# A two-block transformer kernel on one core: where each attention's value products stand on TensorE

## The chip, the cores and the metric

The kernel is one program on one core of a Trainium2 chip. The metric is the device time of one execution in microseconds, as the median of several runs. The program is written engine by engine: TensorE, ScalarE (ACT), VectorE (DVE), GpSimd and the DMA queue of SyncE each have a fixed list of instructions, and they meet only at counting semaphores.

## The reference

Two transformer blocks run one after the other on 512 tokens of width 1024 (the first block adds 16 meta tokens, so it has 528). Everything is float32. The three attentions, which the change touches, are:

```python
# block 1, forgetting attention, 8 heads of 64, causal ("fox")
s = q @ k.T * scale + c[t] - c[s];  p = softmax(s);  o = p @ v
# block 1, stick-breaking attention, 8 heads of 64, causal ("sb")
z = q @ k.T * scale
a = exp(log_sigmoid(z) + later_sum_of(log_sigmoid(-z)));  o = a @ v
# block 2, grouped-query attention, 8 heads on 2 key/value heads, not causal ("gqa")
s = rope(norm(q)) @ rope(norm(k)).T * scale;  p = softmax(s);  o = p @ v
```

Around them stand the input projections, gates, output projections, the two feed-forward nets and, in block 2, a bidirectional mLSTM with a convolution.

## The kernel before, in words

Large products are made in three passes of rounded high and low parts (`three`, L585 to L588). ACT rounds a weight chunk to its high part (`split`, L1578), DVE makes the low part (`split`, L2303), and TensorE waits for the low part.

Each attention is cut into units. A unit is 128 queries of a pair of heads; in fox and sb, which are causal, it has 1 to 4 blocks of 128 keys, and units 0 and 1 are small ones for the last 16 tokens. There are 18 units in fox, 18 in sb and 16 in gqa. One unit goes through these steps:

- scores (S): TensorE, two products of 64 rows each (L768, L888, L1200), in fox and sb followed by 128-row products that add a bias or mask (L771, L773, L891);
- the weights: in fox DVE's least value (L2424), ACT's exponentials (L1721), reciprocal and scaling (L2431, L2433, L1734); in gqa L2788, L1974, L2804, L2806, L1985; in sb sigmoids on ACT and scans on DVE (L1781, L2495, L2499);
- turns T0 and T1 (L790, L909, L1215): transposes of the first and the second head's weights, both into PSUM bank 6, so T1 waits for ACT's copy of T0 (L1729, L1788, L1981), and the next unit's T0 waits for DVE's copy of T1 (L2444, L2508, L2800);
- values (V): TensorE, products into 64 columns each (L824, L928, L1231), summed over the key blocks into bank 7. In fox's and sb's units 0 and 1 they are products of 32 columns (L801). After four units, a pair of heads is complete and ACT and DVE copy it out of bank 7 (in gqa L2087 and L2859).

The loops interleave the steps of neighbouring units with pieces of a large product, the "fill", so that TensorE has work while ACT and DVE make the weights. The order on TensorE in iteration n, with the number of the unit in brackets:

- fox: S(n), T0(n-1), fill, V(n-2), T1(n-1). The fill has 48 products up to n = 8 and 24 for most of the later ones (n = 13 has 64 small ones, L719).
- sb: fill, V(n-2), T0(n-1), S(n+1), T1(n-1).
- gqa: S(u+1), first half of the fill, T0(u), V(u-1), second half, T1(u). After T1(8) come 16 small transposes (L1281); the next fill half waits for ACT's copy of them (L2091).

In gqa, ACT's order in an iteration is: evacuate the last fill, exp(u+1), in some iterations a weight split, copy of T0(u), scale the next weights. DVE's is: greatest of the scores u+1, in some iterations a low-part split, gate or convolution work, reciprocal and scaling of u+1, copy of T1(u). So the copy of T0(u) stands behind the exponentials of the scores that TensorE made at the head of the same iteration.

Of the kernel before, what the change touches and what calls it, by code (L numbers as in the profile page):

```python
# [6 lines left out]
F = mybir.dt.float32  # L7
R = mybir.dt.float32r
ALU = mybir.AluOpType
ACT = mybir.ActivationFunctionType  # L10
# [6 lines left out]
T2 = 512  # L17
# [244 lines left out]
def build(nc, W, XT, VECS, CONS, ROPE, OUT):  # L262
    with ExitStack() as ctx:
# [172 lines left out]
        def bank(b, n, rows=slice(0, P), off=0):  # L436
            return psf[rows, 512 * b + off:512 * b + off + n]
# [7 lines left out]
        def gq_split(u):  # L445

            return AT["o2", 0] + (0 if u == 0 else (u + 1) // 2) if u == 0 or (u % 2 == 1 and u <= 13) else None
# [129 lines left out]
        def _(pe):  # L577
# [199 lines left out]
            def fox_turn(n, x):  # L777

                if x == 0:
                    pe.wait_ge(S["fx_na"], n + 1)  # L780
                    pe.wait_ge(S["fx_pd"], n)
                else:
                    pe.wait_ge(S["fx_nb"], n + 1)
                    pe.wait_ge(S["fx_pa"], n + 1)
                b = fxb[n % 2]
                if n < 2 and x == 1:
                    ins = pe.transpose(bank(6, P, slice(0, 16)), b[:, 1, 0:16], C("id"))
                else:
                    for j in range(4 if n < 2 else (n - 2) % 4 + 1):
                        ins = pe.transpose(bank(6, P, off=128 * j), b[:, x, 128 * j:128 * j + 128], C("id"))  # L790
                ins.then_inc(S["fx_tr"], 1)
# [55 lines left out]
            for n in range(20):  # L847
                if n < 18:
                    fox_scores(n)
                if 1 <= n <= 18:  # L850
                    fox_turn(n - 1, 0)
                if n < 18:
                    fill_a(n)
                if n >= 2:
                    fox_values(n - 2)
                if 1 <= n <= 18:
                    fox_turn(n - 1, 1)


            HQ = (TQ // 2, TQ // 2)  # L860
# [117 lines left out]
            for n in range(20):  # L978
                if n in (2, 3):
                    fill_b(n, (0,))  # L980
                    sb_values(n - 2, range(2))
                    fill_b(n, (1,))
                    sb_values(n - 2, range(2, 4))
                elif n < 19:
                    fill_b(n)
                else:
                    fill_b(n, (0,))
                if n >= 4:
                    sb_values(n - 2)
                if n == 19:  # L990
                    fill_b(n, (1,))
                if 1 <= n <= 18:
                    sb_turn(n - 1, 0)
                if n + 1 < 18:
                    sb_scores(n + 1)
                if 1 <= n <= 18:
                    sb_turn(n - 1, 1)
# [338 lines left out]
            rope_turn(4)  # L1336
            v5_first(1, (2, 3))
            for u in range(17):
                if u < 15:
                    gqa_scores(u + 1)  # L1340
                beside_attention(u, 0)
                if u < 16:
                    gqa_turn(u, 0)
                if u >= 1:
                    gqa_values(u - 1)
                beside_attention(u, 1)
                if u < 16:
                    gqa_turn(u, 1)
                if u == 8:
                    gate_columns()  # L1350
                if u == 15:
                    prep(0, 0)
                    prep(0, 1)
                if u == 16:
                    for piece in (4, 2, 3, 5):
                        prep(0, piece)
# [211 lines left out]
        def _(ac):  # L1568
# [390 lines left out]
            def evac_v5(c, t):  # L1959
                if t % 2:  # L1960
                    ac.wait_ge(S["mm_v5"], 5 + t if c == 0 else 10 + 2 * t)
                    ac.activation(v2[:, t, 322 * c:322 * c + 322], bank(t if c == 0 else (13 + t) % 2, 322), ACT.Copy
                                  ).then_inc(S["ev_v5_a"], 1)
# [96 lines left out]
            rope_eps(4)  # L2060
            gqa_normalise(0)
            evac_v5(0, 3)
            for u in range(17):
                if u >= 1:
                    beside_attention(u - 1)
                if u == 13:
                    split(gq_split(u))
                if u < 15:
                    gqa_exp(u + 1)
                if gq_split(u) is not None and u != 13:  # L2070
                    split(gq_split(u))
                if u == 2:
                    for d in range(2):
                        ac.activation(mrow[d][:, :], con[:, 0:T2], ACT.Copy, scale=0.0).then_inc(S["mr_hi"], 1)
                if u == 6:
                    for d in range(2):
                        ac.wait_ge(S["row_t"], 4 * d + 3)
                        ac.wait_ge(S["mr_hi"], 2)
                        ac.activation(mrow[d][0:4, :], rowt[3 * d + 1][:, :], ACT.Copy).then_inc(S["mr_hi"], 1)
                if u < 16:  # L2080
                    gqa_turned(u)
                if u < 15:
                    gqa_normalise(u + 1)
                if u >= 4 and u % 4 == 0:
                    p = u // 4 - 1
                    ac.wait_ge(S["gq_pv"], 4 * p + 4)
                    ac.activation(yah[:, p, :], bank(7, T2), ACT.Copy).then_inc(S["o_hi"], 1)  # L2087
                if u == 8:
                    ac.wait_ge(S["gt_d"], 6)
                    ac.wait_ge(S["mr_lo"], 2)  # L2090
                    ac.activation(ncol[:, :].rearrange("p (d h i) -> p d i h", d=2, h=4),  # L2091
                                  bank(1, 32, off=32).rearrange("p (d i h) -> p d i h", d=2, h=4), ACT.Exp, scale=-1.0
                                  ).then_inc(S["gt_a"], 5)
                if u == 14:
                    conv_silu((0, 4, 1, 5))
                if u == 15:
                    conv_silu((2, 6, 3, 7))
                    for k in range(4):
                        ac.wait_ge(S["ev_o2"], k + 1)
                        ac.activation(sig[:, k, :], sig[:, k, :], ACT.Tanh, scale=0.5).then_inc(S["o2_s"], 1)  # L2100
                    ac.preload_act_table_set(EXPLN)
                    prep(0, 0)
                    prep(0, 1)
                    split(AT["wo2a", 0])
                if u == 16:
                    beside_attention(16)
# [188 lines left out]
        def _(dv):  # L2295
# [530 lines left out]
            rope_tile(4)  # L2826
            gqa_normalise(0)
            evac_v5(0, 2)
            for u in range(17):
                if u < 15:  # L2830
                    gqa_most(u + 1)
                if gq_split(u) is not None:
                    split(gq_split(u))
                if 1 <= u <= 5:
                    gate_rows(u - 1)
                if u == 5:
                    dv.wait_ge(S["r_y"], 15)
                    for i in range(2):
                        dv.memset(cv[i], 0.0).then_inc(S["cv_z"], 1)
                if 6 <= u <= 13:  # L2840
                    evac_conv(u - 6)
                if 14 <= u:
                    evac_v5(1, u - 14)
                if u < 15:
                    gqa_normalise(u + 1)
                if u < 16:
                    gqa_turned(u)
                if u == 8:
                    dv.wait_ge(S["mm_gt"], 2)
                    dv.tensor_copy(gcol[:, :], bank(1, 32)).then_inc(S["gt_d"], 6)  # L2850
                if u == 16:
                    dv.wait_ge(S["o2_s"], 4)
                    for k in range(4):
                        dv.tensor_scalar(sig[:, k, :], sig[:, k, :], 0.5, 0.5, ALU.mult, ALU.add).then_inc(S["o2_s"], 1)
                    split(AT["wo2a", 0])
                if u >= 4 and u % 4 == 0:
                    p = u // 4 - 1
                    dv.wait_ge(S["o_hi"], 7 + p)
                    dv.tensor_tensor(yal[:, p, :], bank(7, T2), yah[:, p, :].bitcast(F), ALU.subtract  # L2859
                                     ).then_inc(S["o_lo"], 1)  # L2860
                if u == 7:
                    for d in range(2):
                        dv.wait_ge(S["mr_hi"], 3 + d)
                        dv.tensor_tensor(mrow[d][32:36, :], rowt[3 * d + 1][:, :], mrow[d][0:4, :].bitcast(F), ALU.subtract
                                         ).then_inc(S["mr_lo"], 1)
# [455 lines left out]
```

## Time and profile before

| what | value |
|---|---|
| time, median of 3 runs | 1535.72 us (1535.66 to 1537.25) |
| span of the profiled execution | 1536.3 us |
| TensorE matmul busy | 1483.9 us, 97% |
| VectorE busy | 1025.0 us, 67% |
| ScalarE busy | 655.3 us, 43% |
| mean granted TensorE clock | 0.995 |

The profile gives no separate time for the profiled execution; its span from first to last instruction, 1536.3 us, lies between the shown runs. A row of the timeline gives start, length, engine, source line, what is written and read, and a count; several like instructions in a row are merged. Matmul ends are modelled and overlap the next start, so what a piece of work costs TensorE is read from start to start, not from its length. Float32 products with 64 rows or columns appear as two or more matmul records each.

### The profile page before, as it was taken

To read this page: it belongs to the slowest core of one execution; us is meant where nothing else is said; L and a number is where in the kernel's file an instruction comes from. 1 tells how busy PE (TensorE), PEld (TensorE's weight loads), DVE (VectorE), ACT (ScalarE), POOL (GpSimd) and SP (SyncE) were. 2 spreads that over 40 slices of the span, in tenths; PEclk is the share of its full clock that TensorE was granted. 3 is DMA by queue.
4 is the path that set the end of the run, shared out by engine and by line. 5 is a ranking of instruction groups with operands and counts; after the bars stand their busy time and mean duration, and the time that the engine had idled before them with its cause. 6 is when DMAs were issued, how large, how long until landed. Compare 5 with 4: busy or idle time off the path is not lost.

```text
span 1536.3 us, 27973 instructions
## 1 busy us (share of the span) xinstructions
PE 1483.9 (97%) x11804; PEld 1312.1 (85%) x11804; DVE 1025.0 (67%) x1446; ACT 655.3 (43%) x1052; POOL 23.3 (2%) x20
## 2 busy tenths in 40 slices
PE   7999999999998999999999899999989999999998
PEld 7998878889997999999778667768667999998876
DVE  5543447875536977777665776676778888885454
ACT  4433443342334212212343555546646555554343
POOL 0000000000000000000000020000000000000000
PEclk9999999999999999999999999999999999999999
DMA  5131024443232233232344212110112233322222
GB/s 182 57 111 56 15 70 159 149 141 117 97 110 77 103 110 131 103 107 100 131 165 154 73 54 106 55 36 28 42 42 111 83 110 110 111 94 79 91 95 83
DMA packets 37708, 147.76 MB, mean 96 GB/s; under 512 B 4304, under 2 KB 4432, under 8 KB 27856
## 3 DMA queue, kind: packets, MB, share of 16 engines
q1 hardware_dynamic: 36288, 142.76, 26.9%
q8 instruction: 94, 1.54, 0.4%
q10 hardware_dynamic: 1152, 2.16, 0.4%
q0 software_dynamic: 144, 1.05, 0.2%
q14 instruction: 30, 0.25, 0.0%
HBM read 143.86 MB, written 2.10 MB: 95 GB/s over the span
## 4 chain that ended last, share of the span: by engine, by line
PE 82%; DVE 9%; ACT 5%; issue 2%; DMA 1%; POOL 0%; ACTq 0%; DVEq 0%; SPq 0%
PE ps L586 19%; PE ps L588 18%; PE ps L587 18%; PE ps L1527 4%; PE ps L1525 4%; PE ps L1526 4%; ACT t L1578 2%; DVE t L2303 2%; PE ps L622 1%; PE ps L623 1%; PE ps L624 1%; PE ps L1231 1%; DMA t<-in_XT 1%; PE ps L1200 1%; PE ps L790 1%
## 5 line engine op out<-in xcount | busy, mean ns | idle before, releaser
L586 PE MATMUL ps<-t 128*128 128x258 f32 (+4 forms) x2160 | 688.5, 319 | 23.9 <-DVE t L2351 9.1
L588 PE MATMUL ps<-t 128*128 128x258 f32 (+4 forms) x2160 | 677.0, 313 | 0.0
L587 PE MATMUL ps<-t 128*128 128x258 f32 (+4 forms) x2160 | 675.4, 313 | 0.0
L586 PEld LDWEIGHTS ps<-t 128*128 128x128 f32 (+1 forms) x2160 | 406.8, 188 | 68.5 <-issue 16.7
L588 PEld LDWEIGHTS ps<-t 128*128 128x128 f32 (+1 forms) x2160 | 406.6, 188 | 26.9
L587 PEld LDWEIGHTS ps<-t 128*128 128x128 f32 (+1 forms) x2160 | 407.5, 189 | 24.1
L2303 DVE TENSOR_TENSOR t<-t 128x1024 fp32r<-128x1024 f32 (+2 forms) x121 | 205.6, 1699 | 211.5 <-ACT t L1578 211.5
L1578 ACT ACTIVATE t<-t 128x1024 fp32r<-128x1024 f32 (+2 forms) x121 | 174.0, 1438 | 196.2 <-PE ps L588 173.2
L1527 PE MATMUL ps<-t 128*128 128x256 f32 x504 | 142.6, 283 | 0.0
L1525 PE MATMUL ps<-t 128*128 128x256 f32 x504 | 142.5, 283 | 0.1
L1526 PE MATMUL ps<-t 128*128 128x256 f32 x504 | 141.3, 280 | 0.0
L1526 PEld LDWEIGHTS ps<-t 128*128 128x128 f32 x504 | 95.9, 190 | 0.0
L1525 PEld LDWEIGHTS ps<-t 128*128 128x128 f32 x504 | 94.6, 188 | 0.3 <-issue 0.3
L1527 PEld LDWEIGHTS ps<-t 128*128 128x128 f32 x504 | 94.2, 187 | 0.0
L3078 DVE TENSOR_TENSOR t<-t 128x1024 fp32r<-128x1024 f32 (+1 forms) x78 | 78.6, 1014 | 21.2 <-ACT t L2222 21.1
L1894 ACT ACTIVATE t<-t 128x512 f32<-128x512 f32 x22 | 13.9, 632 | 153.0 <-DVE t L2651 153.0
L2222 ACT ACTIVATE t<-t 128x1024 fp32r<-128x1024 f32 (+1 forms) x78 | 68.7, 889 | 7.1 <-PE ps L588 4.2
L2526 DVE SCALAR_TENSOR_TENSOR t<-t 128x512 f32<-128x512 f32 x84 | 62.8, 747 | 4.8 <-DMA t<-in_W 2.0
L2640 DVE TENSOR_TENSOR t<-ps,t 128x516 f32<-128x516 f32 x44 | 30.4, 691 | 43.8 <-PE ps L588 40.6
L2621 DVE TENSOR_TENSOR t<-t 128x512 fp32r<-128x512 f32 x88 | 56.6, 684 | 1.2 <-ACT t L1883 1.2
L1883 ACT ACTIVATE t<-t 128x512 fp32r<-128x512 f32 x88 | 50.0, 617 | 3.2 <-DVE t L2658 3.2
L3066 DVE TENSOR_TENSOR t<-t 128x512 f32<-128x512 f32 x72 | 49.5, 688 | 1.3
(326 smaller groups left out, 1740.8 us busy)
## 6 DMA issues: line engine op xcount, KB each, us to landing
t<-in_W SPq DMA_DIRECT2D x75, 1024.0 KB, 4.8
t<-in_W SPq DMA_DIRECT2D x62, 512.0 KB, 3.3
t<-in_W SPq DMA_DIRECT2D x100, 256.0 KB, 3.7
t<-in_W SPq DMA_DIRECT2D x4, 644.0 KB, 3.8
t<-in_XT ACTq DMA_DIRECT2D x8, 264.0 KB, 8.9
out<-t SPq DMA_DIRECT2D x8, 256.0 KB, 2.7
t<-in_ROPE POOLq DMA_DIRECT2D x1, 1024.0 KB, 5.3
t<-in_CONS SPq DMA_DIRECT2D x1, 423.0 KB, 12.2
```

Source lines behind the costliest of these rows:

```text
L586: pe.matmul(out, wh, xh, start=first, stop=False)
L587: pe.matmul(out, wh, xl, start=False, stop=False)
L588: return pe.matmul(out, wl, xh, start=False, stop=last)
L1525: pe.matmul(out, wh, xh[:, k, :], start=(k == 0 and b in (0, 1)), stop=False, skip_group_check=True)
L1526: pe.matmul(out, wh, xl[:, k, :], start=False, stop=False, skip_group_check=True)
L1527: ins = pe.matmul(out, wl, xh[:, k, :], start=False, stop=(k == 3), skip_group_check=True)
L1578: ac.activation(whi[:, n % 2, o:o + width], wraw[:, n % 2, 0:width], ACT.Copy).then_inc(S["w_hi"], 1)
L2222: ins = ac.activation(wfh[:, at:at + 512 * len(r)], src[:, a:a + 512 * len(r)], ACT.Copy)
L2303: dv.tensor_tensor(wlo[:, n % 2, o:o + width], wraw[:, n % 2, 0:width], whi[:, n % 2, o:o + width].bitcast(F), ALU.subtract).then_inc(S["w ...
L2526: dv.scalar_tensor_tensor(out=x, in0=raw(n)[:, :], scalar=condc[:, k:k + 1], in1=x, op0=ALU.mult, op1=ALU.add).then_inc(S["a_acc"], 1)
L2621: dv.tensor_tensor(al[v % 4][:, :], src[:, v % 22, :], ah[v % 4][:, :].bitcast(F), ALU.subtract).then_inc(S["an_lo"], 1)
L3078: ins = dv.tensor_tensor(wfl[:, at:at + w_], src[:, a:a + w_], wfh[:, at:at + w_].bitcast(F), ALU.subtract)
```

## The change

In fox, the values move from behind the fill to behind T1, so that they stand ahead of the next scores. In sb, they move from ahead of T0 to behind it, ahead of the scores. In gqa, they move from behind T0 to the head of the next iteration, ahead of the scores. The last iterations of each loop keep the old order. In gqa, the values of unit u - 2 now come at the head of iteration u, and ACT's and DVE's copies of a complete pair of heads move from the end of iteration 4p + 4 to iteration 4p + 5: ACT's ahead of the exponentials, DVE's behind the greatest-value reduction and ahead of the split. No instruction is added or removed.

```diff
@@ TensorE, fox
-                if n >= 2:
+                if n == 19:
                     fox_values(n - 2)
                 if 1 <= n <= 18:
                     fox_turn(n - 1, 1)
+                if 2 <= n <= 18:
+                    fox_values(n - 2)
@@ TensorE, sb
-                if n >= 4:
+                if n == 19:
                     sb_values(n - 2)
-                if n == 19:
                     fill_b(n, (1,))
                 if 1 <= n <= 18:
                     sb_turn(n - 1, 0)
+                if 4 <= n <= 18:
+                    sb_values(n - 2)
                 if n + 1 < 18:
                     sb_scores(n + 1)
@@ TensorE, gqa
             for u in range(17):
+                if u >= 2:
+                    gqa_values(u - 2)
                 if u < 15:
                     gqa_scores(u + 1)
                 beside_attention(u, 0)
                 if u < 16:
                     gqa_turn(u, 0)
-                if u >= 1:
+                if u == 16:
                     gqa_values(u - 1)
@@ ScalarE, gqa
+            def gqa_out(p):
+                ac.wait_ge(S["gq_pv"], 4 * p + 4)
+                ac.activation(yah[:, p, :], bank(7, T2), ACT.Copy).then_inc(S["o_hi"], 1)
+
             for u in range(17):
                 if u >= 1:
                     beside_attention(u - 1)
                 if u == 13:
                     split(gq_split(u))
+                if u >= 5 and u % 4 == 1:
+                    gqa_out(u // 4 - 1)
                 if u < 15:
                     gqa_exp(u + 1)
...
-                if u >= 4 and u % 4 == 0:
-                    p = u // 4 - 1
-                    ac.wait_ge(S["gq_pv"], 4 * p + 4)
-                    ac.activation(yah[:, p, :], bank(7, T2), ACT.Copy).then_inc(S["o_hi"], 1)
+                if u == 16:
+                    gqa_out(3)
@@ VectorE, gqa
+            def gqa_low(p):
+                dv.wait_ge(S["o_hi"], 7 + p)
+                dv.tensor_tensor(yal[:, p, :], bank(7, T2), yah[:, p, :].bitcast(F), ALU.subtract
+                                 ).then_inc(S["o_lo"], 1)
+
             for u in range(17):
                 if u < 15:
                     gqa_most(u + 1)
+                if u >= 5 and u % 4 == 1:
+                    gqa_low(u // 4 - 1)
                 if gq_split(u) is not None:
                     split(gq_split(u))
...
+                if u == 16:
+                    gqa_low(3)
```

## Rows read from the trace of the kernel before

**Rows 1.** The page's chain that ended last, shares by engine.
```profile
PE 82%; DVE 9%; ACT 5%; issue 2%; DMA 1%; POOL 0%; ACTq 0%; DVEq 0%; SPq 0%
```

**Rows 2.** Windows over fox, sb and gqa: us, busy of each engine, clock, DMA.
```profile
94.00:220.00 126.00, 122.17 (x1197) 104.95 (x1195) 52.37 (x95) 50.62 (x122) 0.00 (x0) 1.00 0.11 39
220.00:366.00 146.00, 143.10 (x1495) 123.42 (x1492) 104.87 (x140) 57.14 (x87) 0.00 (x0) 1.00 0.46 149
920.00:1077.00 157.00, 154.69 (x995) 115.31 (x996) 110.55 (x170) 84.92 (x154) 5.25 (x3) 1.00 0.17 56
```

**Rows 3.** TensorE timeline, sb: the fill's last product and four transposes right behind.
```profile
234.74 0.29 PE L588 MATMUL ps<-t 128*128 128x258 f32 x1
234.86 0.60 PE L909 MATMUL ps<-t 128*128 128x128 f32 x4
```

**Rows 4.** TensorE timeline, fox: fill, values, four transposes, scores.
```profile
143.68 0.28 PE L588 MATMUL ps<-t 128*128 128x264 f32 x1
143.89 0.88 PE L824 MATMUL ps<-t 128*64 128x128 f32 x12
144.70 0.66 PE L790 MATMUL ps<-t 128*128 128x128 f32 x4
145.29 0.49 PE L768 MATMUL ps<-t 64*128 64x256 f32 x2
```

**Rows 5.** TensorE timeline, fox's last values with sb's first scores behind.
```profile
219.15 1.09 PE L824 MATMUL ps<-t 128*64 128x128 f32 x16 [0.94 <-DVE t L2444]
220.18 0.63 PE L879 MATMUL ps<-t 64*32 64x512 f32 x4
```

**Rows 6.** TensorE timeline, gqa: T0(0) and fill; T0(1), V(0), fill; T1(1).
```profile
935.45 0.60 PE L1215 MATMUL ps<-t 128*128 128x128 f32 x4
935.81 0.48 PE L586 MATMUL ps<-t 128*128 128x512 f32 x1
...
943.17 0.60 PE L1215 MATMUL ps<-t 128*128 128x128 f32 x4
943.70 1.09 PE L1231 MATMUL ps<-t 128*64 128x128 f32 x16
944.73 0.50 PE L586 MATMUL ps<-t 128*128 128x512 f32 x1
...
947.63 0.60 PE L1215 MATMUL ps<-t 128*128 128x128 f32 x4
```

**Rows 7.** Timelines of ACT, DVE, TensorE, fox: T1(12), T1(13) and T0(14).
```profile
193.98 1.92 ACT L1578 ACTIVATE t<-t 128x2048 fp32r<-128x2048 f32 x1 [3.40 <-DMA t<-in_W]
...
198.53 0.68 DVE L2444 COPY t<-ps 128x512 f32<-128x512 f32 x1
...
190.11 0.52 PE L790 MATMUL ps<-t 128*128 128x128 f32 x3 [0.48 <-ACT t L1729]
...
197.22 0.63 PE L790 MATMUL ps<-t 128*128 128x128 f32 x4 [0.79 <-ACT t L1729]
...
199.36 0.30 PE L790 MATMUL ps<-t 128*128 128x128 f32 x1 [0.28 <-DVE t L2444]
```

**Rows 8.** ACT's timeline, gqa: copies of T0(1), T0(2) and T0(6).
```profile
946.50 0.59 ACT L1981 ACTIVATE t<-ps 128x512 f32<-128x512 f32 x1
...
956.58 0.59 ACT L1981 ACTIVATE t<-ps 128x512 f32<-128x512 f32 x1
...
992.33 0.57 ACT L1981 ACTIVATE t<-ps 128x512 f32<-128x512 f32 x1
```

**Rows 9.** Gqa: who waited for whom (us, times, longest); TensorE; DVE's last split.
```profile
PE ps L1215 <- DVE t L2800: 1.1, 3, 0.5
...
1011.98 0.63 PE L1215 MATMUL ps<-t 128*128 128x128 f32 x4 [0.27 <-ACT t L1981]
...
1015.14 0.47 PE L586 MATMUL ps<-t 128*128 128x512 f32 x1 [0.39 <-ACT t L2091]
...
1053.01 1.49 DVE L2303 TENSOR_TENSOR t<-t 128x1288 fp32r<-128x1288 f32 x1
```

More of the change, by code:

```diff
@@ L2855, in _ @@
                     split(AT["wo2a", 0])
[L2856 to L2860, printed above, removed]
+                if u == 16:
+                    gqa_low(3)
                 if u == 7:
```

## The prediction

> **What bounds the kernel now.** I read the page first. The chain that ended last runs 82% over TensorE [rows 1], so time is lost or won where TensorE's own list gets longer or shorter, or where it waits. The windows over the three attentions say the same: TensorE is busy 122.2 of 126 us in fox, 143.1 of 146 in sb and 154.7 of 157 in gqa, at full granted clock [rows 2]. The busy share hides two things that this change touches, and both are read from the timeline, from start to start. One is the price of the edges between kinds of products. The other is the small waits for ACT's and DVE's copies of the transposes. DVE is busy 110.6 of 157 us in gqa [rows 2] and has a fixed order, so there the two side engines can set the pace for a while.
>
> **Part 1: the edges.** No instruction is added, so on TensorE only the neighbours change.
> - From the fill's last start to the values it is 143.89 - 143.68 = 0.21 us [rows 4]; from the fill's last start to transposes 234.86 - 234.74 = 0.12 [rows 3]. Four transposes behind a fill take 0.60 [rows 3], four behind values 0.66 [rows 4].
> - Values of 16 records take 220.18 - 219.15 = 1.03 with scores behind [rows 5] and 944.73 - 943.70 = 1.03 with fill behind [rows 6]. Values to scores is thus an edge like any other: standing side by side saves nothing by itself. What is saved is one edge a unit, since transposes join the fill without one.
> - Fox and sb, before: fill, V, T, S. After: fill, T, V, S. Saved: 0.09 + 0.06 = 0.15 us a unit, say 0.14 with rounding.
> - Gqa, before: T0 0.53, V 1.03, fill half 947.63 - 944.73 = 2.90, T1 [rows 6]. After: T0 to fill is 935.81 - 935.45 = 0.36 [rows 6], V costs its 1.03 behind T1. Saved: 0.17, and some 0.02 in the fill behind; 0.19 a unit.
> - Units with the new order ahead of scores (or of a turn, in sb): fox n = 2 to 16 (the first two with 32-column values, taken at 0.1), sb n = 4 to 18, gqa u = 2 to 14. Gross: 0.2 + 13 x 0.14 = 2.0; 15 x 0.14 = 2.1; 13 x 0.19 = 2.5. Together 6.6 us.
>
> The Trainium skill (TensorEngine Tiling (Array Packing), Key Properties) says that changing the tiling mode drains TensorE; by it too there is one change fewer a unit, not two, which rows 3 to 5 bear out. With the 166 ns that it gives as the warm constant of a single matmul (TensorE: Matmul & The Clock Gate, Single matmul latency) for each, an estimate of the gross is 43 x 0.166 = 7.1 us; the rows give 6.6 and they decide.
>
> **Part 2: waits in fox.** The values used to stand between the fill and T1, where they also passed the time until ACT's copy of T0 was there. Now T1 follows the fill at once. Where that copy is late, T1 waits longer and the values come on top, behind it. In return they stand in front of the next T0, which waits for DVE's copy of T1.
> - T1(12) is at 190.11 because it waited 0.48 for ACT's copy; T1(13) at 197.22, after 0.79 [rows 7]. The second goes back to ACT's weight split at 193.98, which waited 3.40 for a DMA that is released by the small products of iteration 13 [rows 7]. Both T1 stay where they are relative to iteration 13, so the savings of two units are lost here.
> - V(12), 0.81 us (144.70 - 143.89 for the same size [rows 4]), comes behind T1(13) in the open. T0(14) at 199.36 had 0.28 to 0.44 us of waiting for DVE's copy at 198.53 [rows 7]; that absorbs 0.44 of the 0.81, so 0.37 is lost.
> - One more T1, in iteration 9, the first with a short fill, would be ready about 0.25 before its copy. In the tail the copy of T1(16) by DVE starts some 0.46 earlier and the rest of the tail with it, after a stall of 0.25 that this figure contains.
> - Sum for fox: -0.2 - 9 x 0.14 + 0.25 + 0.37 - 2 x 0.14 - 0.46 = -1.6 us.
>
> **Part 3: sb.** ACT's copy of T0 waits for the values too (one buffer), before and after, and starts at the end of whichever comes second. That end lies as far ahead of the scores as before. The DVE products that T0 waits for are done 4 us and more ahead. I see no new wait. At two fills TensorE already waited for DVE behind this copy, and there the 0.14 is not gained. So -13 x 0.14 = -1.8 us.
>
> **Part 4: gqa, where it is given back.** The copy of T0(u) stands on ACT behind the exponentials of S(u+1), the split and other work, a chain that starts at S(u+1). V(u-1) lay between T0(u) and T1(u) and covered most of it. Without V, T1(u) is ready 1.2 us earlier, and where the copy is later than that, the time is lost again and V's 1.03 is still to come. I went through ACT's, DVE's and TensorE's lists unit by unit with the durations of the rows; "shift" is after minus before.
> - T1(1): the copy ends at 946.50 + 0.59 = 947.09 [rows 8]; T1(1) would be ready at 947.63 - 1.2 = 946.4. It starts at 947.2, shift -0.4; V(0) behind it makes S(3) +0.6. T0(2) was one of three that waited for DVE's copy [rows 9], so the shift there is 0. T1(2): the copy ends at 956.58 + 0.59 = 957.17 [rows 8], fixed by DVE's chain; shift 0, and S(4) is at +1.0.
> - Then three units gain 0.19 each: S(7) at +0.4. T1(6) waits for the copy that ends at 992.90 [rows 8] and, since its chain starts from +0.45, for 0.4 more: S(8) at +1.4.
> - T0(8) and T1(8) waited before already, the latter at 1011.98 for ACT [rows 9]; both are tied by DVE's chain to S(8). So T1(8) stays at +1.4, and V(7) behind it makes S(10) +2.4. The fill's wait of 0.4 at 1015.14 [rows 9] goes: +2.0.
> - T0(10) and T1(10) tie it again: S(12) at +2.0; S(14) at +1.65.
> - DVE's last split, 1.49 us at 1053.01 [rows 9], follows the maximum of S(14), which is now late, and in the new order the 0.68 us copy of a complete pair as well. It ends some 2.2 later. The fill half that needs it would be there at +0.4 (V no longer stands ahead of it) and had 0.3 to spare, so it waits 1.5, a new wait. With the V that is still to come behind T1 the end of gqa is at +2.9.
>
> The mLSTM behind it starts from the last fill and copies; nothing there has a fixed time, so the shift stays. The sum: -1.6 - 1.8 + 2.9 = -0.5 us. On the span of 1536.3 that is 1535.8; the median of the runs is 0.6 lower, so I predict 1535.2 us: no change that can be told. The moved copies cost TensorE nothing: bank 7 is needed again only a unit later.
>
> **Rivals.** Chances are in brackets.
> - No change, as above (0.81). Its own range is 1533.7 to 1537.2: the gqa loss is bounded by 1.4 (if the late split hides) and 4 (if the three late copies add up on each other).
> - The savings hold and the waits do not come (0.10): 1535.7 - 6.6 = 1529.1. For it: TensorE waited only some 2 us in gqa's windows, so the side engines look idle enough. Against it: the copies of rows 8 end 0.1 to 0.5 us before the old T1, while T1 comes 1.2 earlier. It turns faster if the gqa loss stays under about 0.3 us.
> - Slower, through gqa's weight splits (0.06): in iterations with a split, ACT and DVE need about as long from S(u+1) to T0(u+1) as TensorE. If each late S starts a later chain and each chain ties T0 and T1 again, every second unit leaves V's 1.03 in the open: gqa loses 7 x 1.03 = 7.2 net, and with the -3.4 of fox and sb the time is 1535.7 + 3.8 = 1539.5. It decides from a gqa loss of 6.5 us on. Against it: with split, the copy in iterations 3, 5, 7 and 9 ends 0.3 to 0.6 us before the new T1.
> - The edge is not saved, since transposes ahead of values drain as the fill did (0.03): +6.6 - 0.5, 1541.8. Rows 3 and 6 speak against it.
>
> **The numbers.** This kernel can be told from no change at about 0.2%, 3.1 us. Faster than 1532.6 has 0.10, slower than 1538.8 has 0.09, same 0.81. The range of 8 in 10 is that of the likeliest case with some room on both sides for the others: 1532.4 to 1538.0.
>
> **What would show it.** In fox and sb, fill's last start to T should read 0.12, V of 16 records 1.03 ahead of scores, and a unit 0.14 less. T1(13) should still wait for ACT, T0(14) not. In gqa, T1(1), T1(2), T1(6) and T1(8) should each show an idle time of 0.8 to 1.4 us released by ACT's copy, a fill half near the end of gqa should wait for DVE's split, and the stage should be some 3 us longer, against 3.4 less in fox and sb together. If gqa is not longer, my chains are wrong; if fox and sb are not shorter, the edges are.

## The result, and the profile after

| | before | after |
|---|---|---|
| median of 21 runs each | 1536.65 us (1535.66 to 1539.07) | 1539.42 us (1535.55 to 1543.11) |
| span of the profiled execution | 1536.3 us | 1537.5 us |
| mean granted clock of that execution | 0.995 | 0.993 |

The ratio after/before is 1.0015, with an interval of 1.0009 to 1.0021. That is between no change and 0.2% slower, and the median, 1539.4, lies above my range of 1532.4 to 1538.0. The same kernel, run again beside the experiments, gave 1.0002 (0.9993 to 1.0011), which is no change. The two intervals overlap only from 1.0009 to 1.0011; why the first came out higher stays open. So no measurement shows a gain; that the whole kernel is slower is shown by the first measurement and not by the repeat. The loss inside gqa, below, is there in every profile of a kernel with the new gqa order.

The page of after has the same busy times and nearly the same chain as [rows 1]:

```profile
PE 1482.6 (96%) x11804; PEld 1314.0 (85%) x11804; DVE 1025.4 (67%) x1446; ACT 655.1 (43%) x1052; POOL 23.3 (2%) x20
...
PE 81%; DVE 9%; ACT 5%; issue 3%; DMA 1%; POOL 0%; ACTq 0%; DVEq 0%; SPq 0%
```

So the change has to be looked for stage by stage. The windows of [rows 2] had round bounds; these go from the first work of a stage to the end of its last values, so that lengths can be compared. The columns are the stretch and its length, busy time (and instructions) of TensorE, of its weight loads, of DVE, ACT and GpSimd, then the granted clock, DMA share and GB/s. First the kernel before, from top to bottom fox, sb and gqa:

```profile
91.66:220.18 128.52, 124.69 (x1220) 106.29 (x1219) 53.09 (x96) 52.53 (x123) 0.00 (x0) 1.00 0.12 45
220.18:364.48 144.30, 141.40 (x1480) 121.89 (x1478) 104.63 (x139) 55.74 (x84) 0.00 (x0) 1.00 0.47 151
919.88:1074.35 154.47, 152.16 (x982) 113.06 (x981) 108.91 (x168) 83.01 (x151) 5.37 (x3) 1.00 0.17 57
```

And the same three of after:

```profile
90.82:217.63 126.81, 122.72 (x1219) 105.84 (x1219) 53.04 (x96) 52.42 (x123) 0.00 (x0) 1.00 0.13 45
217.63:361.69 144.06, 140.75 (x1480) 123.07 (x1479) 104.67 (x139) 55.62 (x84) 0.00 (x0) 0.99 0.48 151
917.13:1075.57 158.44, 151.99 (x982) 112.99 (x981) 109.07 (x168) 83.74 (x151) 5.36 (x3) 0.99 0.16 56
```

Fox is 1.71 us shorter, sb 0.24 shorter and gqa 3.97 longer. Fox starts 0.84 earlier, at 90.82 for 91.66 us; in all ten other profiles of this study it starts between 90.41 and 91.08, so it was before that began late by chance. Between sb and gqa 0.04 is added, and behind gqa nothing that the rounding of the span shows. Together that is the span's +1.2. In gqa TensorE is as busy as before (152.0 against 152.2 us), and its idle time went from 2.3 to 6.5 us. The equal busy time hides two opposite things that come up below: edges that are saved, and a stretch at a lower clock, in which the same products are busy for longer.

The waits of TensorE in the gqa stretch of after say for whom (us in total, times, longest). They answer to [rows 9]:

```profile
PE ps L1218 <- ACT t L1986: 4.2, 4, 1.5
PE ps L1263 <- DVE t L2312: 1.1, 1, 1.1
PE ps L1218 <- DVE t L2809: 0.5, 1, 0.5
```

Behind L850 the line numbers of after are those of before plus 2 to 9: L1986 is ACT's copy of T0 (L1981 before), L1218 the turns, L2809 DVE's copy of T1 and L2312 its split. In the timeline the four are T1(1), T1(2), T1(6) and T1(8). The values and scores behind the first are shown too, and last comes the half fill that waits for DVE's split (start, length, engine, line, operation, count, idle time before and its releaser):

```profile
944.48 0.63 PE L1218 MATMUL ps<-t 128*128 128x128 f32 x4 [0.66 <-ACT t L1986]
945.03 1.09 PE L1234 MATMUL ps<-t 128*64 128x128 f32 x16
946.06 1.13 PE L1203 MATMUL ps<-t 64*128 64x512 f32 x4
...
954.55 0.63 PE L1218 MATMUL ps<-t 128*128 128x128 f32 x4 [1.08 <-ACT t L1986]
...
990.74 0.63 PE L1218 MATMUL ps<-t 128*128 128x128 f32 x4 [1.00 <-ACT t L1986]
...
1010.66 0.63 PE L1218 MATMUL ps<-t 128*128 128x128 f32 x4 [1.49 <-ACT t L1986]
1011.22 1.15 PE L1284 MATMUL ps<-t 4*128 4x4 f32 x16
1012.29 1.26 PE L1234 MATMUL ps<-t 128*64 128x128 f32 x16
1013.48 2.08 PE L1203 MATMUL ps<-t 64*128 64x512 f32 x4
1015.49 0.79 PE L586 MATMUL ps<-t 128*128 128x512 f32 x1
...
1018.86 0.60 PE L1218 MATMUL ps<-t 128*128 128x128 f32 x4
...
1054.99 0.42 PE L1263 MATMUL ps<-t 128*128 128x322 f32 x1 [1.09 <-DVE t L2312]
```

Three things are to be seen. The waits stand where the prediction put them. V costs 946.06 - 945.03 = 1.03 ahead of scores as it did ahead of a fill. And behind T1(8) something stands that I had not foreseen: V(7) takes 1013.48 - 1012.29 = 1.19 instead of 1.03, and the scores of unit 10 take 1015.49 - 1013.48 = 2.01 instead of 946.06 to 947.12, 1.06. The granted clock (the column behind GpSimd's) in windows that follow each other there:

```profile
1009.20:1010.66 1.46, 0.00 (x1) 0.03 (x1) 1.39 (x3) 1.31 (x4) 0.00 (x0) 1.00 0.00 0
1010.66:1012.29 1.63, 1.63 (x20) 1.45 (x20) 1.56 (x4) 0.21 (x1) 0.00 (x0) 1.00 0.04 10
1012.29:1013.48 1.19, 1.19 (x18) 0.86 (x17) 0.98 (x3) 0.64 (x3) 0.00 (x0) 0.83 0.00 0
1013.48:1015.49 2.01, 2.01 (x7) 0.51 (x5) 0.00 (x0) 1.04 (x3) 0.00 (x0) 0.50 0.01 4
1015.49:1018.90 3.41, 3.41 (x15) 2.71 (x14) 1.98 (x3) 1.84 (x5) 0.00 (x0) 0.85 0.00 0
```

TensorE stood still for 1.46 us, did 20 small products, and then had its lower clock (1.2 of 2.4 GHz, 0.50 in the column) for about 3 us. The Trainium skill (TensorE: Matmul & The Clock Gate, Part 1: The HAM clock gate) names 1.2 GHz as the idle and 2.4 GHz as the busy state of the clock; the windows at 0.50 and at 1.00 agree with these two.

Such a stretch stands in sb of after too. The first fence is after, the second the same kernel, run again, over the same window:

```profile
248.00:251.70 3.70, 3.70 (x25) 3.69 (x20) 3.49 (x6) 0.07 (x1) 0.00 (x0) 0.57 0.03 9
```

```profile
248.00:251.70 3.70, 3.70 (x33) 3.70 (x33) 3.49 (x6) 0.10 (x1) 0.00 (x0) 1.00 0.02 6
```

25 products against 33 in the same time. An idle time of TensorE stands ahead of this stretch as well, at small products of 32 columns; here it is in after, and in gqa_only, which is described below:

```profile
247.85 0.24 PE L630 MATMUL ps<-t 128*32 128x1 f32 x6 [1.03 <-issue]
```

```profile
249.65 0.23 PE L630 MATMUL ps<-t 128*32 128x1 f32 x6 [1.07 <-issue]
```

"issue" means that the profile shows nothing that TensorE waited for. In the repeat the same idle time is 0.80 us and the clock stays at 1.00. The length of sb in the two executions, 144.06 against 142.35, puts the whole difference at 1.7 us: 0.23 of it is the longer idle time. The rest is the lower clock: from 248.66 to 251.89 the fill's products start 0.215 us apart instead of 0.12, which costs 1.4.

### The profile page after: what moved, and what is told of

It is laid out like the page before. It is cut to its first block, busy times and chain, and to the rows that moved or that the text cites. A ratio compares the mean times of both kernels' runs of the same rounds, so it can differ in the third digit from the quotient of the medians.

```text
span 1537.5 us, 27973 instructions
## 1 busy us (share of the span) xinstructions
PE 1482.6 (96%) x11804; PEld 1314.0 (85%) x11804; DVE 1025.4 (67%) x1446; ACT 655.1 (43%) x1052; POOL 23.3 (2%) x20
## 3 DMA queue, kind: packets, MB, share of 16 engines
q8 instruction: 94, 1.54, 0.4%
## 4 chain that ended last, share of the span: by engine, by line
PE 81%; DVE 9%; ACT 5%; issue 3%; DMA 1%; POOL 0%; ACTq 0%; DVEq 0%; SPq 0%
PE ps L586 18%; PE ps L588 18%; PE ps L587 18%; PE ps L1532 4%; PE ps L1530 4%; PE ps L1531 4%; DVE t L2312 2%; ACT t L1583 2%; PE ps L622 1%; PE ps L623 1%; PE ps L624 1%; PE ps L1203 1%; PE ps L1234 1%; DMA t<-in_XT 1%; PE ps L768 1%
## 5 line engine op out<-in xcount | busy, mean ns | idle before, releaser
L2312 DVE TENSOR_TENSOR t<-t 128x1024 fp32r<-128x1024 f32 (+2 forms) x121 | 205.7, 1700 | 210.1 <-ACT t L1583 209.9
```

The costliest lines, as they stand in the source:

```text
L2312: dv.tensor_tensor(wlo[:, n % 2, o:o + width], wraw[:, n % 2, 0:width], whi[:, n % 2, o:o + width].bitcast(F), ALU.subtract).then_inc(S["w ...
```

## The experiments

Three theories stood against each other for gqa's 4 us. **A**: the waits alone, each late copy with V's 1.03 behind it, as in the prediction. **B**: the waits give about 2.9, and the rest is the lower clock that follows the long wait at T1(8). **C**: the loss is not in gqa's order at all, but in fox and sb, whose saved edges are given back.

### The change in halves

`gqa_only` has fox and sb in the order of before:

```diff
-                if n == 19:
+                if n >= 2:
                     fox_values(n - 2)
...
-                if 2 <= n <= 18:
-                    fox_values(n - 2)
...
-                if n == 19:
+                if n >= 4:
                     sb_values(n - 2)
...
-                if 4 <= n <= 18:
-                    sb_values(n - 2)
```

> Only gqa in the new order. Theory of waits (T1 stands in front of ACT's copies that the values used to cover): the gqa stage is 4 us longer than before, with four idle times of ACT's copies ahead of T1 and one of DVE's split, and a half-clock stretch behind T1(8); the kernel is 3 to 4 us slower. Rival, the clock alone: the waits cost nothing by themselves, and the stage is longer only by the half-clock stretch, 1.6 us. Rival, fox or sb is what slows the changed kernel: this one is no slower than before.

`fox_sb` has gqa's values and the copies of its pairs where they were before:

```diff
             for u in range(17):
-                if u >= 2:
-                    gqa_values(u - 2)
...
-                if u == 16:
+                if u >= 1:
                     gqa_values(u - 1)
@@ ScalarE and VectorE: the copies of a pair
-                if u >= 5 and u % 4 == 1:
-                    gqa_out(u // 4 - 1)
...
-                if u == 16:
-                    gqa_out(3)
+                if u >= 4 and u % 4 == 0:
+                    ... # the same copy, p = u // 4 - 1
```

> Fox and sb in the new order, gqa in the old. Theory of waits: fox 1.75 us shorter, sb 1.85 shorter, the kernel 3.4 us faster, and no half-clock stretch in sb. Rival, the clock: the new order in sb brings the half-clock stretch seen at 248 us, so that sb gains next to nothing, and the kernel is 1.5 to 2 us faster.

`after_again` is the changed kernel, unedited, on the same chip as both.

> The changed kernel once more, for a second profile and as a measure beside the others. If the half-clock stretches in sb (248 us) and behind T1(8) in gqa (1012 us) belong to the order of the work, both are there again; if they are chance, they are elsewhere or gone. Time 2 to 3 us over before by the theory of waits with the one behind T1(8) fixed.

| kernel | median, us | runs | ratio to before (interval) | fox | sb | gqa |
|---|---|---|---|---|---|---|
| before | 1537.93 | 27 | 1 | 128.52 | 144.30 | 154.47 |
| gqa_only | 1541.95 | 8 | 1.0024 (1.0014 to 1.0034) | 128.52 | 146.07 | 158.59 |
| fox_sb | 1535.03 | 11 | 0.9982 (0.9973 to 0.9991) | 126.68 | 142.21 | 154.44 |
| after_again | 1538.52 | 11 | 1.0002 (0.9993 to 1.0011) | 126.72 | 142.35 | 158.89 |

The stage lengths are those of one profiled execution each, by windows as above (those of before are the rows shown). For gqa, the window of gqa_only and the window of fox_sb:

```profile
919.98:1078.57 158.59, 151.96 (x981) 113.09 (x980) 109.06 (x168) 83.74 (x151) 5.36 (x3) 0.99 0.16 56
```

```profile
914.62:1069.06 154.44, 152.14 (x981) 113.11 (x981) 108.96 (x168) 82.95 (x151) 5.36 (x3) 1.00 0.16 57
```

C falls. Fox and sb alone gain 1.84 and 2.09 us in the profile and 0.18% in the runs; gqa alone loses 4.12 in the profile and 0.24% in the runs. The halves add up to 1.0006, between the two measurements of the whole. gqa_only also has the stretch at the lower clock at 250 us, in sb, in the old order (146.07 for 144.30): the new order is not needed for it.

### The long wait at T1(8)

Three kernels shorten or fill the wait ahead of T1(8), each in another way, and a fourth leaves it as it is. `v7_old` leaves only V(7) where it was, between T0(8) and T1(8):

```diff
+EARLY = (0, 1, 2, 3, 4, 5, 6, 8, 9, 10, 11, 12, 13, 14)
...
-                if u >= 2:
+                if u - 2 in EARLY:
                     gqa_values(u - 2)
...
-                if u == 16:
+                if u >= 1 and u - 1 not in EARLY:
                     gqa_values(u - 1)
```

(ACT's and DVE's copies of a pair go by the same list.)

> The changed kernel with the values of gqa unit 7 alone back in their old place (and the copies of their complete pair too). They cover T1(8)'s wait again, which falls from 1.43 us to 0.2. Theory of waits: scores 10 start 1.0 us earlier, of which 0.5 is left at the end of gqa. Theory that the half-clock stretch behind T1(8) comes with the long wait ahead of it: scores 10 take 1.06 us again instead of 2.01 and 1.6 us more come back, gqa is 2.0 us longer than before instead of 4. Rival, the stretch belongs to the values and scores side by side behind the small transposes: scores 10 still take 2.0 us.

`gate_first` puts the 16 small transposes ahead of T1(8), so that they pass the time:

```diff
-                if u < 16:
-                    gqa_turn(u, 1)
                 if u == 8:
                     gate_columns()
+                if u < 16:
+                    gqa_turn(u, 1)
```

> The changed kernel with the 16 small transposes of the gates ahead of T1(8) instead of behind it, so that they lie in its wait. Theory of waits: the wait of 1.4 us falls to 0.4, and gqa is 1.1 us shorter than in the changed kernel. If the half-clock stretch comes from the empty time, it goes too, and gqa is 2.7 us shorter; if small products of 4 columns count as empty time for the clock, the stretch stays, somewhat earlier.

`filled` leaves the order of the change alone and puts one product into the wait. Its result goes into a bank of PSUM that is free there and is used by nothing, so this work is extra:

```diff
+                if u == 8:
+                    pe.wait_ge(S["cv_c"], 3)
+                    pe.matmul(bank(1, T2), C("perm"), qk2[:, 0, :], start=True, stop=True)
                 if u < 16:
                     gqa_turn(u, 1)
```

> The changed kernel with one product added on TensorE ahead of T1(8), 128 rows by 128 by 512, whose result is not used (it goes to bank 1 and is overwritten by the gates' transposes). It fills 0.85 of the 1.43 us that T1(8) waits and moves nothing else. If the half-clock stretch comes from the empty time ahead of it, scores 10 take 1.1 to 1.5 us instead of 2.0 and the gqa stage is 1.6 us shorter than in the changed kernel, with more work in it. Rival, the stretch comes from the small transposes and the scores behind: no change. Theory of waits alone: no change either.

The timeline of filled answers to the rows of after at 1010.66:

```profile
1008.21 1.02 PE L1354 MATMUL ps<-t 128*128 128x512 f32 x2
1009.86 0.63 PE L1218 MATMUL ps<-t 128*128 128x128 f32 x4 [0.63 <-ACT t L1989]
1010.42 1.15 PE L1284 MATMUL ps<-t 4*128 4x4 f32 x16
1011.50 1.09 PE L1234 MATMUL ps<-t 128*64 128x128 f32 x16
1012.52 1.13 PE L1203 MATMUL ps<-t 64*128 64x512 f32 x4
1013.58 0.51 PE L586 MATMUL ps<-t 128*128 128x512 f32 x1
...
1016.49 0.60 PE L1218 MATMUL ps<-t 128*128 128x128 f32 x4
```

From the small transposes to T0(9) it takes 1016.49 - 1010.42 = 6.07 us; in after it was 1018.86 - 1011.22 = 7.64. Nothing in that stretch differs but the clock: the added product lies ahead of it, and T1(8) starts when ACT's copy lets it, 93.51 us behind the start of the stage for 93.53 in after. So the lower clock costs 1.57 us here, and an unused product that fills the wait gives them back.

How much of the 1.57 reaches the end of gqa depends on where the stretch begins. T0(10) is tied to the scores of unit 10 by DVE's chain: it starts 12.28 us behind their end (the start of what follows them) in after, in after_again and in low_behind (below), and 12.29 in filled. These scores end 1.13 us later in after than in filled, and 1.61 later in after_again, where the clock fell earlier (V(7) takes 1.70 there and 1.19 in after). What falls behind the scores is taken up by T0(10), which waits 0.47 for DVE in filled and shows no wait in after. So gqa as a whole is 1.14 us shorter in filled than in after, and 1.59 shorter than in after_again; 1.6 was expected.

V(7) in its old place (v7_old) leaves an idle time of 0.27, and the scores' records are as short as before, 1.13. Gqa is 2.24 us longer than in before, for the 2.0 that the clock theory gave:

```profile
1009.99 0.63 PE L1219 MATMUL ps<-t 128*128 128x128 f32 x4 [0.27 <-ACT t L1987]
1010.55 1.15 PE L1285 MATMUL ps<-t 4*128 4x4 f32 x16
1011.63 1.13 PE L1204 MATMUL ps<-t 64*128 64x512 f32 x4
```

And with the transposes first (gate_first) an idle time of 0.41 remains, and V(7) takes 1.02. Gqa is 2.23 shorter than in after and 2.68 shorter than in after_again, for the expected 2.7:

```profile
1009.60 1.15 PE L1284 MATMUL ps<-t 4*128 4x4 f32 x16
1011.16 0.63 PE L1218 MATMUL ps<-t 128*128 128x128 f32 x4 [0.41 <-ACT t L1986]
1011.72 1.09 PE L1234 MATMUL ps<-t 128*64 128x128 f32 x16
1012.74 1.13 PE L1203 MATMUL ps<-t 64*128 64x512 f32 x4
```

The fourth, `low_behind`, aims at the other end of gqa. It moves DVE's copy of the third pair behind the split at u = 13, for which a half fill waits, and leaves T1(8) alone:

```diff
-                if u >= 5 and u % 4 == 1:
+                if u in (5, 9):
                     gqa_low(u // 4 - 1)
                 if gq_split(u) is not None:
                     split(gq_split(u))
+                if u == 13:
+                    gqa_low(2)
```

> The changed kernel, with DVE's copy of the third complete pair behind the last split instead of ahead of it. Theory of waits: the split ends 0.6 us earlier, the wait of the fill half in iteration 13 falls from 1.1 to 0.5 us, and the end of gqa comes 0.2 to 0.6 us earlier, since the copy then delays DVE's convolution work. Rival, that wait is the split's own lateness and not the copy's: no change there.

```profile
1053.08 0.42 PE L1263 MATMUL ps<-t 128*128 128x322 f32 x1 [0.49 <-DVE t L2312]
```

| kernel | median, us | ratio (interval) | gqa | idle ahead of T1(8) | scores of unit 10 to the next start |
|---|---|---|---|---|---|
| after | 1539.42 | 1.0015 (1.0009 to 1.0021) | 158.44 | 1.49 | 2.01 |
| v7_old | 1537.22 | 0.9999 (0.9989 to 1.0009) | 156.71 | 0.27 | 1.54 |
| gate_first | 1536.99 | 0.9995 (0.9986 to 1.0005) | 156.21 | 0.41 | 1.58 |
| filled | 1537.49 | 1.0002 (0.9992 to 1.0011) | 157.30 | 0.63 | 1.06 |
| low_behind | 1537.96 | 1.0008 (0.9999 to 1.0018) | 158.73 | 1.49 | 1.80 |

(The 1.54 and 1.58 contain the fill's wait for ACT's copy of the small transposes, as before had it in [rows 9]. Kernels two to five had 10 runs each. Each ratio is to the runs of before beside it, whose median was 1536.65 for after, 1536.91 for filled and 1537.11 for the other three, so the ratios are to be compared and not the medians.) B holds: all four kernels that stand still for the whole 1.5 us ahead of T1(8), after, after_again, gqa_only and low_behind, have the stretch at the lower clock, and none of the other seven profiled kernels has it. The length of a wait doesn't decide alone, though: behind T1(2) and T1(6), which waited 1.08 and 1.00 us in after, the clock stays at 1.00. Whether 1.46 us of standing still would do it without the 20 small products behind was not tried. The remaining 2.8 us of filled (157.30 - 154.47) are the waits of theory A. By the runs alone none of v7_old, gate_first and filled can be told from before or from after_again; it is the profile that tells them apart.

low_behind was a miss. The half fill's wait fell from 1.09 to 0.49 as meant, but I had expected the end 0.2 to 0.6 earlier. The fair comparison is after_again, which has the same wait of 0.47 at T0(10): 158.73 against 158.89, so 0.16 is left of the 0.6. T1(14) waits 0.18 for ACT's copy and starts 0.3 us later behind T0(14) than it did: the wait moved on along the chain.

### Which values may move

`keep5` leaves V(1), V(5), V(7), V(11) and V(12) in the old place. Lines as in v7_old, with

```diff
+EARLY = (0, 2, 3, 4, 6, 8, 9, 10, 13, 14)
```

> The changed kernel with the values of gqa units 1, 5, 7, 11 and 12 back in their old place: those whose move opened a wait. Theory of waits: T1(1) still waits 0.7 to 0.9 us (nothing covered it but the values of unit 0), the waits of T1(2), T1(6), T1(8) and of the fill half of iteration 13 are gone or as small as before, no half-clock stretch, and the gqa stage is as long as before, within 0.3 us. Ten values are still in the new place. Rival, the new place itself costs time: the stage is 2 us or more longer than before.

`mixed` leaves all in the old place but five, those that no late copy stands behind, and V(0), which costs one small wait:

```diff
+EARLY = (0, 2, 3, 4, 10)
```

> Fox and sb in the new order; in gqa only the values of units 0, 2, 3, 4 and 10 are moved, those that no late copy stands behind. Theory of waits: the gqa stage is 0.8 us shorter than before, all in all 4.2 us faster than before. Rival: if any moved values cost time in gqa, the stage is longer than before.

The gqa stage of keep5, and that of mixed:

```profile
915.70:1070.01 154.31, 151.06 (x981) 112.58 (x980) 109.04 (x168) 83.65 (x151) 5.36 (x3) 1.00 0.16 57
```

```profile
918.39:1072.12 153.73, 151.26 (x981) 112.92 (x980) 109.07 (x168) 83.12 (x151) 5.37 (x3) 1.00 0.17 57
```

keep5 is 0.16 us shorter than before in gqa and has a median of 1533.91 (ratio 0.9979, 0.9970 to 0.9988). Of its ten moved values V(13) and V(14) have no scores behind them and save no edge; the other eight should save 8 x 0.19 = 1.5 by my price. Only four do. V(2), V(3) and V(4) bring T0(8) 0.60 us forward against before, and V(10) brings the 0.60 to 0.77 at T0(13). V(0) gains nothing, since T0(2) starts when it did before. V(6) and V(8) run into DVE's copies: T0(8) waits 0.55 for 0.35, T0(10) 0.46 for 0.26. T1(14), which did not wait before, waits 0.32 for ACT's copy, and at T0(15) 0.21 is left. mixed is 0.74 shorter in gqa, which is four edges of 0.19 (V(0) gains nothing there either). Its ratio is the lowest: 0.9975 (0.9965 to 0.9985; median 1533.46 of 8 runs), with fox and sb as changed. Between mixed, keep5 and fox_sb (0.9982) the intervals decide nothing; all three beat both kernels of the study.

## Why the prediction was off

**The edges were right.** Fox: predicted -1.6, measured -1.71 (-1.84 in fox_sb). Sb: predicted -1.8, measured -2.1 in fox_sb and -1.95 in after_again; in after itself the chance stretch hid it. T1(13) waits for ACT and T0(14) does not, as said in Part 2, and V(12) behind it takes 0.80 for the predicted 0.81. Rows of after that answer to [rows 7] (L1734 is ACT's copy of T0 in after, L1729 in before):

```profile
187.95 0.52 PE L790 MATMUL ps<-t 128*128 128x128 f32 x3 [1.07 <-ACT t L1734]
...
195.07 0.63 PE L790 MATMUL ps<-t 128*128 128x128 f32 x4 [1.61 <-ACT t L1734]
195.63 0.88 PE L824 MATMUL ps<-t 128*64 128x128 f32 x12
196.43 0.70 PE L768 MATMUL ps<-t 64*128 64x256 f32 x4
...
197.58 0.29 PE L790 MATMUL ps<-t 128*128 128x128 f32 x1
```

The saving is one edge a unit, not two, as Part 1 read from the rows. The rival that the edge is not saved is out by fox_sb.

**The waits in gqa were right.** The prediction named T1(1), T1(2), T1(6), T1(8) and the half fill near the end, and put their net price at +2.9. filled, which has them all (T1(8)'s is partly filled, but T1(8) starts no earlier) and no lower clock, measures 157.30 - 154.47 = +2.8. The single idle times came at 0.66, 1.08, 1.00 and 1.49 us for "0.8 to 1.4", two of them just outside, and the half fill waited 1.09 for 1.5. Along the stage the chain of Part 4 can be followed turn by turn. It put T1(1) at -0.4, T1(2) at 0, T1(6) at +0.4 and T1(8) at +1.4; measured are -0.40, -0.01, +0.38 and +1.43. It put the unit behind at +2.0; T0(9) and T0(10) of filled are at +1.99 and +2.01. So the rival that the waits do not come is out, and so is the one in which every weight split ties a unit: gqa would have lost 7.2. That this rival's 1539.5 is the measured median is chance: it needed a loss of 6.5 us or more in gqa, and gqa lost 4.0. (The likeliest case's own range had a slip: a gqa loss of 4 gives 1535.7 - 3.4 + 4 = 1536.3, not 1537.2.)

**First step that failed: Part 4's sum at T1(8).** There I moved T1(8) to +1.4 and V(7) behind it at 1.03, and took the work behind as long as before. I priced the wait by its length alone and put the clock behind it at nothing. The wait is followed by the lower clock, which costs up to 1.6 more. gqa's term should have read +2.9 + 1.6 = +4.5; measured are +3.97, +4.12 and +4.42, where 0.5 of the 1.6 can be taken up at T0(10). This is shown by filled, which changes only what fills the wait, and by v7_old and gate_first. With it the sum is -0.5 + 1.6 = +1.1 us, or +0.07%, beside +0.06% from the two halves.

**Second: the base.** I took 1535.7, the median of three runs, for the level of the kernel. The 21 runs of before have a median of 1536.65, 0.9 above it. From 1536.65, the same sum of -0.5 would have given 1536.2, and with the missed 1.6 it gives 1537.8. I also compared the profiled span of 1536.3 with the times of the runs, as if it lay between them. In each of the 21 runs of after the time is the span plus 1.8 to 1.9 us, and so it is in the later runs of before (1.7 to 1.9). The profiled execution of before was thus one of about 1538.2, some 1.5 above the median. That did not move the forecast, because the 0.6 taken off led back to the 1535.7.

**Third: the width of the range.** The runs of after lie between 1535.55 and 1543.11. Their spans go with the clock: 1533.7 us at a mean granted clock of 0.996, 1541.2 at 0.990. I took my range from the unknown terms of the sum alone. One source is seen: in 4 of the 11 profiles (before and ten of others) sb is 1.7 to 3.4 us longer than in the others with its order, one of them of gqa_only, where sb's code has the old order. In after, gqa_only and mixed the stretch behind L630 is in it. In mixed and gate_first a fill also waits 1.72 and 2.29 us instead of 0.43, because ACT's weight split waited for a DMA, and in gate_first a stretch at the lower clock follows this wait. Other such stretches, at about 465 and 860 us, are in all 11.

The profiled execution of after took 1539.42, which is the median, and it is one with the stretch in sb. So 1.7 us of its time are that, as much as separates 1539.4 from 1537.8. In how many of the 21 runs of either kernel it occurred is not recorded, so whether it explains the median stays open. The repeat does not confirm a missing part: it is 0.6 us slower than the before beside it, where the corrected sum says 1.1. With an interval of 1.4 us to each side it fits that sum and the forecast of -0.5 alike; it is the profiles that show the missed term.

## What to carry to other kernels

Work that stands between a producer and its consumer on the bounding engine also covers the copy between them. Before it is moved, compare unit by unit when the copy ends with when the consumer would be ready, and move only the units that have room: in gqa five moved values saved 0.7 us, and all fifteen cost 4. A wait of 1.5 us on TensorE can cost twice its length, since a slower clock may follow; one extra product inside it was free here. And a forecast of half a per mille needs the level of the kernel before from more than three runs.

## What was unexpected of the hardware

- After 1.46 us without a product and about 1.6 us of 20 small ones, the granted clock went from 1.00 to 0.50. It came back within the 3.4 us of the last window, and in all 1.57 us were lost. With an idle time of 0.63 (filled), 0.41 (gate_first) or 0.27 (v7_old) at the same place it stayed at 1.00.
- The same idle time can be followed by the lower clock in one execution and not in another. At L630 in sb TensorE stands still for 0.75 to 1.08 us in every profile. The stretch at 0.50 followed in after, gqa_only and mixed (1.03, 1.07 and 1.07) and not in v7_old and filled (1.07 and 1.08), nor in the six with 0.75 to 0.80. In mixed even 1.72 us, at 328 us, was followed by a clock of 1.00. What decides was not found.
- The stretches at 465 and 860 us, too, come with idle times of TensorE: in after 3.85 us, and 1.61 and 1.70 us.
- Products into 64 columns with 64-row products behind take 1.03 us for 16 records ([rows 5], and 945.03 to 946.06 in after), as with full ones behind ([rows 6]).
